# Layer b's attention units dealt to other slots: head groups 1 and 2 start one slot later, the three-tile units of a known group one slot sooner

## What is computed

```
def dsa_attention(q, k, v, q_idx, k_idx, w_idx):          # per block of 128 queries
    iscore = relu(einsum('bqhd,bsd->bqhs', qib, k_idx))   # 8 index heads of 64
    iscore = einsum('bqh,bqhs->bqs', wb, iscore)
    iscore = where(admissible, iscore, NEG)
    _, sel = top_k(iscore, 128)                           # 128 keys per query
    logits = q . k[sel] * 128**-0.5 - slope[head] * |qpos - sel|
    p = softmax(where(valid, logits, NEG))
    out = p . v[sel]                                      # ATT_HEADS = 12
```

## Time and profile before

| | |
|---|---|
| median of 3 runs | 1652.65 us (1652.22 to 1652.96) |
| the profiled execution's own time | 1652.55 us |
| its span | 1650.8 us, so 1.75 us lie around it |
| TensorE clock granted, mean | 0.999 |
| PE busy | 1627.0 us (99%) |
| PE weight loads | 1381.9 us (84%) |
| DVE busy | 1046.3 us (63%) |
| ACT busy | 664.6 us (40%) |
| GpSimd busy | 1039.3 us (63%) |

### The profile page before, as it was taken

How to read it: one execution, slowest core, us unless ns; L and a number is a source line. 1 busy time by engine, 2 the same in 40 slices (tenths; PEclk the granted TensorE clock), 3 DMA queues, 4 the chain that set the end, 5 groups by cost and what they waited for, 6 DMA issues and landing times.

```text
span 1650.8 us, 23774 instructions
## 1 busy us (share of the span) xinstructions
PE 1627.0 (99%) x8755; PEld 1381.9 (84%) x8755; DVE 1046.3 (63%) x1634; ACT 664.6 (40%) x1166; POOL 1039.3 (63%) x788
## 2 busy tenths in 40 slices
PE   6999999999999999999999999999999999999998
PEld 5898897888978999999988888887878778877887
DVE  5323948773537745745757997999656786556624
ACT  5422237420324523623544446765312245555301
POOL 7676764566647784784765888784467643334664
PEclk9999999999999999999999999999999999999999
DMA  6333333322243242342334323222233222111231
GB/s 212 118 114 104 128 103 105 100 94 90 98 153 102 77 129 76 103 128 78 102 103 128 91 88 102 77 77 77 93 137 110 77 77 77 52 51 52 77 115 64
DMA packets 188347, 162.59 MB, mean 98 GB/s; under 512 B 7636, under 2 KB 184400, under 8 KB 187728
## 3 DMA queue, kind: packets, MB, share of 16 engines
q1 hardware_dynamic: 188040, 161.10, 30.7%
q10 hardware_dynamic: 200, 0.06, 0.0%
HBM read 155.87 MB, written 4.23 MB: 97 GB/s over the span
## 4 chain that ended last, share of the span: by engine, by line
PE 93%; DVE 4%; ACT 1%; DMA 1%; issue 1%; POOL 0%; DVEq 0%; SPq 0%; ACTq 0%
PE g_bank L1046 54%; PE g_bank L1420 10%; PE g_bank L1080 6%; PE g_bank L1070 5%; PE g_bank L1483 2%; PE t_bank L1420 2%; PE t_bank L1759 2%; PE g_bank L1629 1%; PE t_bank L1771 1%; PE t_bank L1371 1%; PE t_bank L1403 1%; PE t_bank L1748 1%; PE t_bank L1547 1%; PE t_bank L1568 1%; PE g_bank L1611 1%; PE t_bank L1304 1%
## 5 line engine op out<-in xcount | busy, mean ns | idle before, releaser
L803 POOL TENSOR_SCALAR w_hi<-w_raw 128x2048 fp32r<-128x2048 f32 x67 | 132.6, 1979 | 387.3 <-PE g_bank L1046 160.9
L820 POOL TENSOR_TENSOR w_lo<-w_raw,w_hi 128x512 fp32r<-128x512 f32 x264 | 367.0, 1421 | 5.5
L1046 PE MATMUL g_bank<-x_hi,w_hi 128*128 128x512 f32 x912 | 364.5, 400 | 0.4 <-DVEq L2633 0.4
L1046 PE MATMUL g_bank<-x_hi,w_lo 128*128 128x512 f32 x912 | 355.4, 390 | 0.0
L1046 PE MATMUL g_bank<-x_lo,w_hi 128*128 128x512 f32 x912 | 355.2, 389 | 0.0
L1046 PEld LDWEIGHTS g_bank<-x_hi,w_hi 128*128 128x128 f32 x912 | 171.3, 188 | 38.9 <-issue 4.8
L1046 PEld LDWEIGHTS g_bank<-x_hi,w_lo 128*128 128x128 f32 x912 | 171.2, 188 | 36.1
L1046 PEld LDWEIGHTS g_bank<-x_lo,w_hi 128*128 128x128 f32 x912 | 171.4, 188 | 35.2 <-issue 1.4
L3175 DVE SCALAR_TENSOR_TENSOR t_bank<-hc,cols,t_bank 128x512 f32<-128x512 f32 x280 | 187.0, 749 | 4.9 <-DVE hc L3159 3.0
L954 POOL TENSOR_TENSOR w_lo<-w_raw,w_hi 128x512 fp32r<-128x512 f32 x100 | 127.3, 1305 | 67.7 <-ACT w_hi L2279 67.7
L1046 PE MATMUL g_bank<-y_hi,w_hi 128*128 128x512 f32 x288 | 113.5, 394 | 0.0
(11 more groups left out here) (565 smaller groups left out, 3983.5 us busy)
## 6 DMA issues: line engine op xcount, KB each, us to landing
w_raw<-w_gate_up SPq DMA_DIRECT2D x44, 512.0 KB, 4.8
w_raw<-a_w_in SPq DMA_DIRECT2D x44, 512.0 KB, 4.4
w_raw<-b_w_in SPq DMA_DIRECT2D x38, 512.0 KB, 4.3
w_raw<-w_in SPq DMA_DIRECT2D x28, 512.0 KB, 4.5
w_raw<-w_kv SPq DMA_DIRECT2D x16, 512.0 KB, 4.3
w_raw<-w_out_mix SPq DMA_DIRECT2D x16, 512.0 KB, 6.3
w_raw<-w_down SPq DMA_DIRECT2D x16, 512.0 KB, 4.4
w_raw<-a_w_out SPq DMA_DIRECT2D x16, 512.0 KB, 4.3
```

The lines of the kernel that those rows point to most:

```text
L803: nc.gpsimd.tensor_scalar(w_hi[:, par], w_raw[:, par], 1.0, 0.0, ALU.mult, ALU.add).then_inc(pool_chain, 1)
L820: last = nc.gpsimd.tensor_tensor(w_lo[:, par, s], w_raw[:, par, s], w_hi[:, par, s].bitcast(F32), ALU.subtract)
L1046: last = nc.tensor.matmul(g_bank[:, 2 * pair + f if banks is None else banks[f], 0:n], ww[:, k0 + k, ws], xk, start=(k == 0 and q == 0), s ...
```

## The change

Two edits. The table deals the units to other slots: (2, 0) goes from slot 3 to slot 2 and the pair of head group 1 from slot 2 to slot 3; (2, 1) goes from slot 5 to slot 4 and the pair of head group 2 from slot 4 to slot 5. Slots 0, 1 and 6 to 12 keep the logits they have. With the units move their transposes (two slots later) and their values (three slots later). `p_unit` then has to lay a pair out in `pB2` too, since pairs now stand in odd slots.

```diff
-SLOT_UNITS = [[(0, 0)], [(1, 0)], [(0, 1), (1, 1)], [(2, 0)], [(0, 2), (1, 2)], [(2, 1)], [(2, 2)], [(3, 0)], [(3, 1)], [(3, 2)]]
+SLOT_UNITS = [[(0, 0)], [(1, 0)], [(2, 0)], [(0, 1), (1, 1)], [(2, 1)], [(0, 2), (1, 2)], [(2, 2)], [(3, 0)], [(3, 1)], [(3, 2)]]
...
             n, w = SLOT_OF[u], W_OF[UNITS[u][0]]
-            if n % 2:
-                return pB2[i][:, 0:w]
+            ring = [pB2[k][:] if n % 2 else pB[:, k, :] for k in range(4)]
             if len(SLOT_UNITS[n]) == 1:
-                return pB[:, i, 0:w]
-            return pB[:, 0, i * P:(i + 1) * P] if u == units_of(n)[0] else pB[:, 1 + i // 2, i % 2 * w:(i % 2 + 1) * w]
+                return ring[i][:, 0:w]
+            return ring[0][:, i * P:(i + 1) * P] if u == units_of(n)[0] else ring[1 + i // 2][:, i % 2 * w:(i % 2 + 1) * w]
```

## The result

The changed kernel takes 1656.13 us (median of 15 runs, 1652.94 to 1656.69), the kernel before in the same runs 1652.23 us (15 runs, 1650.83 to 1652.96): 3.9 us more, a ratio of 1.0021 with a 95% interval of 1.0013 to 1.0028. So it is slower, by about 0.2%, and by about twice what the sum of the prediction said (+1.8 us).

A forecast was written before the change was run, and what follows sets the result against it. The prediction took PE, busy in 99% of the span, as the bound. From the profiled run's 1652.55 us, -0.93 (query waits) + 0 (exchange) + 2.75 (new stall) = +1.8 us gave 1654.4 us, range 1651.5 to 1655.8.

The forecast's parts named there:

- Part 1: Ends of slots 2 and 4: PE's logits no longer wait for ACT's query copies, a gain of 0.93 us.
- Part 2: Pairs in slots 3 and 5: costs PE nothing, but DVE's later work, including the reciprocal, comes 1.06 us later.
- Part 3: Slot 6: PE's third transposes wait for ACT's values copy to free a bank, a new stall of 2.75 us.
- the fifth task: Slot 6: two values tasks plus three transposes on four banks, so the third transpose reuses the first values bank.
- the two links before it: DVE's reciprocal of slot 5 comes 1.06 us later; ACT's mem_prob waits for it and holds back the values copy.
- The sum: Whole kernel: gain of 0.93, nothing for the exchange, stall of 2.75, together +1.8 us, 1654.4 us; chance 0.75.
- rival B: Slot 6, behind the stall: TensorE's clock halves for the rest of the job, 5.3 us more, 1659.7 us; chance 0.07.

The follow-up runs named there:

- values_first: Changed kernel with ACT doing mem_prob of slots 1, 3 and 5 in the next slot, behind its values copies; 1651.27 us, ratio 0.9995 against the kernel before.
- first_pair: Kernel before with only (2, 0) and the pair of head group 1 exchanged between slots 2 and 3; 1653.54 us, ratio 1.0007.
- second_pair: Kernel before with only (2, 1) and the pair of head group 2 exchanged between slots 4 and 5; 1651.66 us, ratio 0.9999.
- rounds_sooner: Changed kernel with two top-k rounds on DVE moved from slot 5 to slot 4; 1651.88 us, ratio 0.9996 against the kernel before.
- again: The changed kernel measured once more, nothing edited; 1655.53 us, ratio 1.0017 against the kernel before.
- rounds_later: Changed kernel with one top-k round on DVE moved from slot 6 to slot 5; 1659.19 us, ratio 1.0039 against the kernel before.

## Why the prediction came out as it did

**Part 1, the two waits: right.** 4.16 us measured, 4.17 forecast, from slot 6's row as the template. The gain of 0.93 us is the lead of values_first (0.93 us by the medians, 0.87 us in the profile).

**Part 2, the pairs: right in kind, a little off in size.** The pair's logits took 2.63 us against 2.58 for the unit, which I had put at nothing. DVE's stretch over the pair was 5.11 us, not 4.76. Between two of its operations the pair of slot 5 left DVE idle for 0.63 us. Slot 5's unit had such a hole before too (0.64 us), and I had taken the pair's time from slot 4 without it. The reciprocal thus stood 13.02 us after the logits' start instead of the 11.82 us that the same PE timeline of before gives: 1.2 us later, not 1.06.

**Part 3, the stall: right**, in its place, its chain and its size: 2.87 us against 2.75. Slots 4 and 8 showed no wait, as said. first_pair and second_pair show the fifth task, rounds_sooner and values_first the two links before it.

**The sum was the wrong one to call likeliest.** The structural sum of +1.8 us stands at +2.0 in the profiles. The time did not end there, since rival B, to which I gave 0.07, happens in most executions by the medians. The step that failed is the weighing of the gap: I set 2.75 us between an idle stretch of 2.35 us that did no harm and one of over 4 us that did, and let the distance to the nearer row decide. Neither row could carry that.

The first is no row at which the clock held, for the clock was not up yet. This is what follows the sixteen transposes of 12.79 in the profile of before, the next matmul and the next group of transposes of the same line:

```profile
16.11 0.77 PE L1220 MATMUL g_bank<-x_hi,w_hi 128*128 128x512 f32 x1
...
17.87 0.60 PE L1139 MATMUL t_bank<-ident,xn_nat 128*128 128x128 f32 x4
```

From 12.79 to 16.11 us the sixteen take 0.21 us each; the four at 17.87 take 0.09 us each (the next matmul starts at 18.22), and slot 6's twelve 0.10 us each. In "again" the first matmuls of 128x512 there follow each other at 0.43 us (17.00, 17.43), the spacing of half clock. The trace's record of the granted clock begins only where it comes up, at 16.74 us in the profile of before, and the column prints 1.00 where there is no record: the 1.00 of rows 15 in the window 12.00 to 16.50 says nothing. The second row, the end of the span, is sound: there the clock did hold for 4.4 us without a matmul before it fell. But it was one draw of a delay that runs from 2.2 to 5.1 us in the profiles, and the same gap of 2.64 us in slot 6 came out both ways.

Rival B's price was off too, the other way: 5.3 us for a whole job at half clock, where 3.4 us at half cost 1.6 us. With the right price B would have read 1656.0 us, near both medians (1656.13 and 1655.53). The time of 1656.13 us lies 0.3 us above the range's upper end, 1655.8, which left B outside; the forecast of a change within 0.2% is just missed by the first set (0.21%) and just met by the second (0.17%).

The Trainium skill's warning against idle gaps between bursts of matmuls, in "TensorE: Matmul & The Clock Gate", section "Why this matters for your kernels", is borne out by rounds_later, with its gap of 4.15 us. The gaps that the section warns of are longer than the 2.64 us of "again", and there the clock fell all the same; the measurement decides. No run showed the fall behind the gap of 1.48 us.

## What to carry to other kernels

When work moves between stages that share a rotating ring of banks, count the tasks of every later stage that inherits a piece of it, not only of the stage that gets it: the cost here came three slots after the edit, where a fifth task met four banks. Then ask what the engine that must free the bank is doing at that moment; in strict order a wait for something unrelated (here the memory heads' reciprocal) holds the bank too, and moving that wait behind the release was worth 4 us in a kernel where the change itself could give 0.9. And price a new idle stretch of TensorE not only by its length, but also by a fall of the clock behind it: here none was seen behind 1.48 us, it came in some executions behind 2.64 and 3.0 us, and by the mean clock in all five behind 4.15 us. Before a row is used to show that the clock held, check by the spacing of the matmuls that it was up at all.

## What the runs showed of the hardware that was not expected

- Behind the same gap of 2.64 us TensorE's granted clock fell in one profile of the changed kernel and stayed up in three. When it fell, it stood at half for 3.4 us and cost 1.6 us.
- Behind a gap of 3.0 us (2.99 in the trace) it fell after PE had resumed, again for 3.4 us; behind 4.15 us it fell inside the gap and stood at half for 6.8 us. Behind 1.48 us it was not seen to fall, in the profile or in the mean clock of 11 executions.
- After the last matmul of the program the clock fell to half 2.2 to 5.1 us later, in 13 profiles.
- Near the start the clock column reads 1.00 while matmuls run at half clock: 0.43 us between 128x512 matmuls at 17.0 us in "again", where the record of the clock begins at 18.07 us.
- At half clock 128x512 matmuls followed each other at 0.43 us, at full clock at 0.23 us.
